# Two heads of 64 tokens in a gathered slot, and the weighted sum on the two column halves of the array

## The chip, the core and the metric

The kernel runs on one core of a Trainium2 chip. Its engines work beside each other and meet at semaphores: TensorE (PE in the profile; its weight loads are PEld), VectorE (DVE), ScalarE (ACT), GpSimd (POOL) and SyncE (SP, which only issues transfers here). Sixteen DMA engines move data between HBM and the core's memory. The metric is the device time of one execution in microseconds (us); less is better.

## The reference, cut to what matters

One layer of a streaming encoder on 1024 prompt tokens and 64 sample tokens, model width 1024. Two branches (a state-space scan and a causal convolution) are gated, merged and added to x. Then comes the part that this case is about: a mixture of 16384 tiny experts. For each token and each of 8 heads the best 16 experts are found from two sets of 128 keys, and each chosen expert contributes one row of `v_tab`, weighted by a softmax and by the gelu of a dot product with its row of `u_tab`:

```python
xn = rmsnorm(x, norm_ffn)
q = (xn @ w_q).reshape(tokens, 8, 2, 128)
s1, s2 = q[:, :, 0] @ keys1.T, q[:, :, 1] @ keys2.T        # tokens, heads, 128
v1, i1 = top_k(s1, 16); v2, i2 = top_k(s2, 16)
sc, pos = top_k(v1[..., :, None] + v2[..., None, :], 16)    # of 256 candidates
eidx = expert number of pos; g = softmax(sc)
coef = g * gelu(einsum('thkd,td->thk', u_tab[eidx], xn))
x = x + einsum('thk,thkd->td', coef, v_tab[eidx])
y = rmsnorm(x, norm_final)
```

All is float32. Every token takes 8 x 16 = 128 expert rows of 2 x 1024 numbers.

## The kernel before, in words

**Two streams of work.** The tokens pass through the layer (called `mix`) in 4 groups of 256 prompt tokens and 16 sample tokens, each group in 64 turns. The expert part (`peer`) works on tiles of 128 tokens: 8 prompt tiles and one tile with the 64 sample tokens. Group 0 runs `mix` alone. Then a loop of three passes runs `mix` of group g + 1 and `peer` of tiles 2g and 2g + 1 turn by turn. What is left, tiles 6, 7 and the sample tile (number 8), runs `peer` alone (`last_tiles`). In a turn k, PE has the products of the layer (L529 most of them; L547 and L557 in the scan stage, turns 10 to 25), then the expert work of four slots.

**A slot.** POOL gathers 128 rows of the expert table (u and v of an expert stand in one row of 8 KB), one per partition, by indices in `idx` (L1306). So a slot is 1 MB: the k-th expert of one head for 128 tokens. `rows` holds a ring of 8 slots. When a slot has landed, DVE multiplies its u half with the normed tokens `xn` and sums each row to one number in `dots` (L1199). For every two slots ACT takes the gelu (L809), DVE multiplies with the softmax weights (`coef`, L1186), and ACT writes for each slot a diagonal matrix `diag` (L812). PE multiplies `diag` with the v half of the rows and adds to `ps_acc` (L673): two matmuls of 512 columns each, with `diag` 128 x 128 as weights, so that `ps_acc` holds 128 tokens by 1024 columns. `slot_free` then lets POOL gather the next. Work is grouped by pairs of heads: a pair `n` has 32 slots, `a` = 0 or 1 says which of the two heads, and DVE chooses the experts of pair n + 1 (`key_top`, `pair_top`, `experts_of`) while pair n is summed, in eight turns.

**The sample tile** has 64 tokens. There the partitions hold two heads of 64 tokens already, `x2t` holds the tokens twice, and `fold` (two unit matrices one above the other) takes the place of `eye` in `diag`, which adds the two heads up.

**Begin and end of a tile.** `start` loads the tile's tokens (`x2t`, by SP), DVE makes `xn` (L1214), and PE puts x into `ps_acc` (L664). `end` waits for all slots: ACT squares `ps_acc` and sums (L825), DVE and ACT make the root (L1220, L827, L1222), and DVE writes `yt` (L1223). PE's `start` of the next tile waits for that. In mid group (turn 32) `end` of the even tile stands among DVE's work on the odd one.

**What sets the order.** The order on each engine is the order of the code; there is no scheduler. SP has one queue: the weight slabs of the layer (`ring`, four slots, L363), the scores that `mix` has stored (`sc`, L379), the tiles' tokens, and the stores of y. `HEAD_LOADS` says in which turns SP waits for the stored scores of a head before it loads them.

## Time and profile before

| | us |
|---|---|
| median of 3 runs | 3884.04 |
| lowest and highest | 3872.71, 3890.49 |
| span of the profiled execution | 3882.3 |
| PE busy | 3333.6 (86%) |
| DVE busy | 2776.0 (72%) |
| POOL busy | 1746.5 (45%) |
| ACT busy | 996.4 (26%) |
| mean granted clock of TensorE | 0.943 |

The profile gives no other time of the profiled execution than its span, from the first instruction to the last. Busy time is the time in which an engine has an instruction of the program at work; a PE record's end is modelled, so records overlap, and what a matmul costs in a row of them is read from the starts. A matmul in float32 leaves two records. The granted clock is 1.0 at 2.4 GHz and 0.5 at 1.2 GHz. The DMA share is the mean busy share of the sixteen DMA engines. By time the kernel has group 0 (0 to about 409 us, where the first slot is used), the loop (to about 3049) with a pass of about 880 us for each group, and the last tiles, which end about 3383, 3715 and 3882.

### The profile page before, as it was taken

What the parts mean: (1) busy time and instruction counts of PE and PEld (TensorE: products, weight loads), DVE (VectorE), ACT (ScalarE), POOL (GpSimd) and SP (SyncE); (2) the same over time, 40 slices, a digit from 0 to 9 for tenths busy, and PEclk for the clock granted to TensorE, in tenths of its full rate; (3) what the DMA queues carried; (4) which work ended last, traced back from release to release, by engine and by line L of the source; (5) the groups of instructions that cost most, each with busy time, mean ns of one, the idle gap of its engine ahead of it and who ended that gap; (6) DMA issues with size and microseconds to landing.
All of it is one profiled execution on the core that took longest, in us unless ns stands there. A gap on an engine that the chain in (4) does not pass through costs nothing.

```text
span 3882.3 us, 38138 instructions
## 1 busy us (share of the span) xinstructions
PE 3333.6 (86%) x9740; PEld 1810.3 (47%) x9740; DVE 2776.0 (72%) x6814; ACT 996.4 (26%) x2429; POOL 1746.5 (45%) x1548
## 2 busy tenths in 40 slices
PE   7878898898989799988999798888989777777777
PEld 5566454454555355454555354444545332233222
DVE  7952579997655569997655569997655677677775
ACT  1012233333222233333222233333222222212222
POOL 1600357744333347754333347854333344444443
PEclk9989999999999899999999899989999999999999
DMA  3235898899999898899999898889999999999998
GB/s 136 77 134 177 329 365 328 310 357 389 409 346 394 321 364 329 334 356 387 403 351 393 322 369 314 341 332 388 402 347 395 368 419 419 384 416 416 419 392 353
DMA packets 232123, 1337.74 MB, mean 345 GB/s; under 512 B 27936, under 2 KB 45472, under 8 KB 92656
## 3 DMA queue, kind: packets, MB, share of 16 engines
q0 software_dynamic: 156672, 1140.92, 74.0%
q1 hardware_dynamic: 63024, 181.13, 12.7%
q10 hardware_dynamic: 12224, 13.38, 1.0%
q8 instruction: 79, 1.29, 0.1%
q14 instruction: 124, 1.02, 0.1%
HBM read 1312.89 MB, written 22.44 MB: 344 GB/s over the span
## 4 chain that ended last, share of the span: by engine, by line
PE 39%; DVE 29%; DMA 15%; issue 11%; ACT 3%; POOL 3%; ACTq 0%; POOLq 0%; DVEq 0%; SPq 0%
PE ps_acc L673 22%; DMA rows<-in_experts,idx 15%; PE ps_a L529 11%; DVE rows L1199 9%; DVE va L1036 4%; PE ps_v L529 4%; POOL rows L1306 2%; DVE gp L1013 2%; DVE cand L1156 1%; DVE coef L1186 1%; DVE cand L1158 1%; PE ps_a L585 1%; DVE part L1160 1%; DVE rin L1002 1%; ACT diag L812 1%
## 5 line engine op out<-in xcount | busy, mean ns | idle before, releaser
L673 PE MATMUL ps_acc<-rows,diag 128*128 128x512 f32 x4352 | 2088.6, 633 | 427.7 <-ACT diag L812 427.7
L1306 POOL DMA_INDIRECT rows<-in_experts,idx x1088 | 1325.1, 1218 | 1864.1 <-PE ps_acc L673 1579.0
L1199 DVE CUSTOM_DVE_ANT_0 rows<-rows,xn 128x1024 f32<-128x1024 f32 x1088 | 1337.7, 1253 | 500.8 <-DMA rows<-in_experts,idx 494.3
L673 PEld LDWEIGHTS ps_acc<-rows,diag 128*128 128x128 f32 x4352 | 853.4, 202 | 1583.4 <-issue 946.1
L529 PE MATMUL ps_a<-xnT,ring 128*128 128x272 f32 x3072 | 747.0, 399 | 6.2 <-DMA ring<-in_slabs 2.7
L529 PEld LDWEIGHTS ps_a<-xnT,ring 128*128 128x128 f32 x3072 | 590.2, 193 | 186.8 <-issue 67.4
L812 ACT ACTIVATE diag<-pk,coef 128x128 f32<-128x128 f32 x1088 | 377.4, 394 | 1135.8 <-DVE coef L1186 1135.8
L809 ACT ACTIVATE act_v<-dots 128x2 f32<-128x2 f32 x544 | 110.5, 203 | 1122.3 <-DVE dots L1199 1118.4
L1036 DVE SCALAR_TENSOR_TENSOR va<-va,pk 128x302 f32<-128x302 f32 x480 | 258.8, 608 | 0.0
L1186 DVE TENSOR_TENSOR coef<-act_v,soft 128x2 f32<-128x2 f32 x544 | 109.7, 202 | 156.8 <-ACT act_v L809 126.0
L529 PE MATMUL ps_v<-uy,ring 128*128 128x272 f32 x512 | 129.0, 402 | 9.8 <-DVE uy L1103 9.8
L809 ACT ACT_TABLE_LOAD x100 | 128.3, 1283 | 13.9 <-issue 12.2
L529 PEld LDWEIGHTS ps_v<-uy,ring 128*128 128x128 f32 x512 | 100.2, 196 | 37.1 <-DVE uy L1103 10.1
L1013 DVE TENSOR_TENSOR_SCAN gp<-rho,carry,rin 128x256 f32<-128x256 f32 (+1 forms) x256 | 107.3, 481 | 0.0
L1199 DVE DVE_READ_ACCUMULATOR2_ANT dots<- 128x1 f32 x1088 | 89.1, 82 | 0.0
L547 PE MATMUL ps_v<-uy,bst 32*128 32x272 f32 x256 | 79.0, 421 | 10.9 <-DVE rot L1004 10.9
L557 PE MATMUL ps_y<-hst,cst 128*32 128x272 f32 x256 | 74.1, 414 | 9.3 <-POOL carry L1287 9.3
L1279 POOL TENSOR_TENSOR hst<-gp 128x272 f32<-128x272 f32 x64 | 72.7, 1136 | 9.4
L585 PE MATMUL ps_a<-pk,sig 128*128 128x128 f32 (+1 forms) x384 | 61.9, 284 | 17.2 <-ACT sig L792 17.2
L1129 DVE MAX8 topv<-sc 128x8 f32<-128x128 f32 x136 | 39.4, 289 | 41.1 <-DMA sc<-score_rows 40.9
L529 PE MATMUL ps_a<-uy,ring 128*128 128x272 f32 x256 | 65.9, 402 | 2.8 <-ACT uy L763 2.8
L792 ACT ACTIVATE sig<-ps_a 128x272 f32<-128x272 f32 x64 | 24.9, 389 | 164.6 <-PE ps_a L529 164.6
(188 smaller groups left out, 2214.3 us busy)
## 6 DMA issues: line engine op xcount, KB each, us to landing
ring<-in_slabs SPq DMA_DIRECT2D x260, 512.0 KB, 7.7
rows<-in_experts,idx POOLq DMA_INDIRECT x1088, 10.1
trig<-trig_rows SPq DMA_DIRECT2D x52, 272.0 KB, 2.9
sc<-score_rows SPq DMA_DIRECT2D x68, 128.0 KB, 6.9
score_rows<-uy ACTq DMA_DIRECT2D x32, 256.0 KB, 6.6
xt<-in_x_prompt SPq DMA_DIRECT2D x5, 1024.0 KB, 9.3
trig_rows<-rows SPq DMA_DIRECT2D x1, 4352.0 KB, 15.2
x_rows<-xt ACTq DMA_DIRECT2D x4, 1024.0 KB, 7.1
```

The source lines that it names most:

```text
L529: last = pe.matmul(out[:, 0:N], w, rhs[:, k, :], start=(k == 0), stop=(k == kt - 1))
L547: pe.matmul(out[:, 0:N], bst[q:q + 32, c, t, :], uT[q:q + 32, t, :], start=True, stop=True).then_inc(v_ready, 1)
L557: last = pe.matmul(ps_y[q:q + 32, 0:N], cst[:, c, j, :], hst[:, j % 2, c, :], start=(c == 0), stop=(c == 1))
L585: last = pe.matmul(out[0:width, t * KEYS:(t + 1) * KEYS], qT[:, m % 2, n:n + width], keys, start=True, stop=True)
L673: ins = pe.matmul(ps_acc[:, h, :], diag[:, slot, :], rows[:, slot, D + h * 512:D + (h + 1) * 512], start=False, stop=False, skip_group_che ...
L809: act.activation(act_v[:, cols], dots[:, cols], ACT.Gelu).then_inc(gelu_done, 1)
L812: act.activation(diag[:, s % RING, :], shape[0], ACT.Copy, scale=coef[:, s:s + 1]).then_inc(diag_done, 1)
L1013: last = dve.tensor_tensor_scan(grot[:, j % 2, p, lo:hi], rho[:, j:j + 1].to_broadcast([P, hi - lo]), rin[:, p, lo:hi], carry[:, p, j, str ...
L1036: last = dve.scalar_tensor_tensor(acc[:, c, :], src, wk, acc[:, c, :], ALU.mult, ALU.add)
L1186: dve.tensor_tensor(coef[:, cols], act_v[:, cols], flat(soft[:, :, :])[:, cols], ALU.mult).then_inc(coef_done, 1)
L1199: ins = dve.tensor_tensor_reduce(rows[:, slot, 0:D], rows[:, slot, 0:D], xn[:, :], 1.0, 0.0, ALU.mult, ALU.add, dots[:, s:s + 1])
L1306: pool.indirect_dma_start(out=rows[:, slot, :], out_offset=None, in_=experts, in_offset=bass.IndirectOffsetOnAxis(ap=idx[:, a, k:k + 1], a ...
```

## The change

A slot now holds two heads of 64 tokens for the prompt tiles too, as it did for the sample tile. `a`, which said which head of the pair, says now which half of the tile's tokens. For every slot `fold` (128 x 64) is scaled to a `diag` of 128 x 64, and its product has only 64 output rows. The two matmuls of a slot go to different halves of the array's columns: columns 0 to 511 of the result to partitions 0 to 63 of `ps_acc`, columns 512 to 1023 to partitions 64 to 127, both in the bank of the token half j. What follows from the new layout: `xn` is kept twice, for each token half on both partition halves (four operations on DVE instead of one); the sum of squares of a token is in two parts that DVE adds across the halves; `yt`, `gl` and the stores of y are in column halves; the scores of a slot's two heads are loaded by two transfers; and the score loads wait for pairs of heads (`PAIR_LOADS`).

```diff
-HEAD_LOADS = {TURNS - 10: 0, TURNS - 7: 1, TURNS - 2: 2}
+PAIR_LOADS = {TURNS - 10: 0, TURNS - 2: 1}
...
-        xn = sb("xn", [P, D])
+        xn = sb("xn", [P, 2, D])
-        yt = sb("yt", [P, D])
+        yt = sb("yt", [P, 2, DH])
-        diag = sb("diag", [P, RING, P])
+        diag = sb("diag", [P, RING, HT])
...
+        halves = (slice(0, HT), slice(HT, P))
+        def half_tiles(t):
+            return 1 if isinstance(t, int) and t == TILES else 2
+        def half_of(n, a):
+            return 0 if isinstance(n, int) and n >= TILES * TPAIRS else a
...
             def load_scores(n, a):
-                sp.dma_start(sc[:, a, :], score_d[2 * n + a]).then_inc(score_in[a], 16)
+                for f in range(2):
+                    sp.dma_start(sc[halves[f], a, :], score_d[2 * n + f, halves[a], :]).then_inc(score_in[a], 16)
...
-                sp.dma_start(y_t[t], yt[:, :]).then_inc(y_out, 16)
+                for f in range(2):
+                    sp.dma_start(y_t[t, f], yt[halves[f], :, :]).then_inc(y_out, 16)
...
-                    if k in HEAD_LOADS:
-                        h = HEAD_LOADS[k]
-                        sp.wait_ge(score_out[h % 2], 128 * g + 128 + 32 * (h // 2 + 1))
-                        pass_wait()
+                    if k in PAIR_LOADS:
+                        for b in range(2):
+                            sp.wait_ge(score_out[b], 128 * g + 128 + 32 * (PAIR_LOADS[k] + 1))
+                            pass_wait()
...
             def start(t):
-                for h in range(2):
-                    last = pe.matmul(ps_acc[:, h, :], eye[0:w, :], x2t[0:w, h * 512:(h + 1) * 512],
-                                     start=True, stop=False, skip_group_check=True)
+                for j in range(js):
+                    for f in range(2):
+                        last = pe.matmul(ps_acc[halves[f], j, :], eye[0:w, halves[j]], x2t[0:w, f * DH:(f + 1) * DH],
+                                         start=True, stop=False, skip_group_check=True)
...
             def peer(n, r, last=False):
                 for s in range(STEPS * r, STEPS * r + STEPS):
-                    slot = s % RING
+                    slot, j = s % RING, half_of(n, s // TOPK)
                     pe.wait_ge(diag_done, PAIR * n + s + 1)
-                    for h in range(2):
-                        ins = pe.matmul(ps_acc[:, h, :], diag[:, slot, :], rows[:, slot, D + h * 512:D + (h + 1) * 512],
+                    for f in range(2):
+                        ins = pe.matmul(ps_acc[halves[f], j, :], diag[:, slot, :],
+                                        rows[:, slot, D + f * DH:D + (f + 1) * DH],
                                         start=False, stop=False, skip_group_check=True)
                     ins.then_inc(slot_free, 1)
...
-                        act.activation(diag[:, s % RING, :], shape[0], ACT.Copy, scale=coef[:, s:s + 1]).then_inc(diag_done, 1)
+                        act.activation(diag[:, s % RING, :], fold, ACT.Copy, scale=coef[:, s:s + 1]).then_inc(diag_done, 1)
...
-                act.activation(yt[:, :], flat(ps_acc[:, :, :]), ACT.Square, accum_out=fin[:, 0:1]).then_inc(y_sq, 1)
+                for j in range(2):
+                    sq_j = act.activation(yt[:, j, :], ps_acc[:, j, :], ACT.Square, accum_out=fin[:, 0, j:j + 1])
+                sq_j.then_inc(y_sq, 1)
...
-                dve.scalar_tensor_tensor(xn[:, :], x2t[:, :], rst[:, 0:1], gf[:, :], ALU.mult, ALU.mult).then_inc(xn_ready, 1)
+                for j in range(half_tiles(t)):
+                    for f in range(2):
+                        last = dve.scalar_tensor_tensor(xn[halves[f], j, :], x2t[halves[j], :], rst[halves[j], 0:1],
+                                                        gf[halves[j], :], ALU.mult, ALU.mult)
+                last.then_inc(xn_ready, 1)
...
-                dve.tensor_scalar(fin[:, 1:2], fin[:, 0:1], 1.0 / D, EPS, ALU.mult, ALU.add).then_inc(y_ms, 1)
+                dve.tensor_scalar(fin[halves[0], 3, :], fin[halves[1], 0, :], 1.0 / D, EPS, ALU.mult, ALU.add)
+                step(dve.tensor_scalar(fin[halves[1], 3, :], fin[halves[0], 0, :], 1.0 / D, EPS, ALU.mult, ALU.add))
+                dve.scalar_tensor_tensor(fin[:, 1, :], fin[:, 0, :], 1.0 / D, fin[:, 3, :], ALU.mult, ALU.add).then_inc(y_ms, 1)
                 dve.wait_ge(y_std, 1 * t + 1)
-                step(dve.reciprocal(fin[:, 3:4], fin[:, 2:3]))
-                dve.scalar_tensor_tensor(yt[:, :], flat(ps_acc[:, :, :]), fin[:, 3:4],
-                                         gl[:, :], ALU.mult, ALU.mult).then_inc(y_ready, 1)
+                step(dve.reciprocal(fin[:, 3, :], fin[:, 2, :]))
+                for j in range(2):
+                    last = dve.scalar_tensor_tensor(yt[:, j, :], ps_acc[:, j, :], fin[:, 3, j:j + 1], gl[:, :],
+                                                    ALU.mult, ALU.mult)
+                last.then_inc(y_ready, 1)
```

The order of the instructions on PE stays. In the loop, turns 4 to 6, before (L529 are the layer's products, L673 a slot's two matmuls, the size is that of the result):

```order
229 L671 REGISTER_ALU
230 L673 MATMUL ps_acc<-rows,diag 128x512 x2
231 L510 REGISTER_ALU
232 L529 MATMUL ps_a<-xnT,ring 128x272 x8
233 L510 REGISTER_ALU
234 L529 MATMUL ps_a<-xnT,ring 128x272 x8
235 L671 REGISTER_ALU
236 L673 MATMUL ps_acc<-rows,diag 128x512 x2
237 L671 REGISTER_ALU
238 L673 MATMUL ps_acc<-rows,diag 128x512 x2
```

and the same place now, where L690 is the slot's line and L544 the layer's:

```order
229 L688 REGISTER_ALU
230 L690 MATMUL ps_acc<-rows,diag 64x512 x2
231 L525 REGISTER_ALU
232 L544 MATMUL ps_a<-xnT,ring 128x272 x8
233 L525 REGISTER_ALU
234 L544 MATMUL ps_a<-xnT,ring 128x272 x8
235 L688 REGISTER_ALU
236 L690 MATMUL ps_acc<-rows,diag 64x512 x2
237 L688 REGISTER_ALU
238 L690 MATMUL ps_acc<-rows,diag 64x512 x2
```

Nothing moved; the slots' products have 64 rows and stand between full ones of 128.

On DVE the end of a prompt tile in the last tiles and the begin of the next, before:

```order
L1220 TENSOR_SCALAR fin<-fin 128x1
L1222 RECIPROCAL fin<-fin 128x1
L1223 SCALAR_TENSOR_TENSOR yt<-ps_acc,fin,gl 128x1024
L1214 SCALAR_TENSOR_TENSOR xn<-x2t,rst,gf 128x1024
```

and now:

```order
L1240 TENSOR_SCALAR fin<-fin 64x2
L1241 TENSOR_SCALAR fin<-fin 64x2
L1242 SCALAR_TENSOR_TENSOR fin<-fin 128x2
L1244 RECIPROCAL fin<-fin 128x2
L1246 SCALAR_TENSOR_TENSOR yt<-ps_acc,fin,gl 128x512 x2
L1232 SCALAR_TENSOR_TENSOR xn<-x2t,rst,gf 64x1024 x4
```

Two small operations and three long ones are more than before, and `yt` is made in two pieces.

## Rows read from the trace of the kernel before

**Rows 1.** The page: busy time, and groups by line (count, busy us, mean ns, idle)
```profile
PE 3333.6 (86%) x9740; PEld 1810.3 (47%) x9740; DVE 2776.0 (72%) x6814; ACT 996.4 (26%) x2429; POOL 1746.5 (45%) x1548
...
L673 PE MATMUL ps_acc<-rows,diag 128*128 128x512 f32 x4352 | 2088.6, 633 | 427.7 <-ACT diag L812 427.7
...
L812 ACT ACTIVATE diag<-pk,coef 128x128 f32<-128x128 f32 x1088 | 377.4, 394 | 1135.8 <-DVE coef L1186 1135.8
```

**Rows 2.** Last tiles by stretches: length, busy PE, PEld, DVE, ACT, POOL; clock, DMA share, GB/s
```profile
3361.00:3392.00 31.00, 20.73 (x34) 7.81 (x35) 19.40 (x47) 9.32 (x21) 6.73 (x7) 0.78 0.88 352
3392.00:3703.00 311.00, 238.87 (x498) 95.14 (x497) 223.24 (x585) 63.33 (x193) 141.60 (x124) 0.96 1.01 414
3703.00:3725.00 22.00, 14.23 (x25) 5.30 (x24) 14.55 (x35) 8.09 (x16) 5.04 (x5) 0.77 0.78 320
```

**Rows 3.** Groups by line, 3392 to 3703 us: the dot products and their wait
```profile
L1199 DVE CUSTOM_DVE_ANT_0 rows<-rows,xn 128x1024 f32<-128x1024 f32 x123 | 149.0, 1225 | 71.8 <-DMA rows<-in_experts,idx 71.1 <-DVE soft L1180 0.6
```

**Rows 4.** One pass of the loop by stretches, columns as in Rows 2
```profile
1303.00:1334.00 31.00, 25.89 (x69) 11.46 (x69) 23.55 (x59) 8.78 (x26) 18.65 (x12) 0.94 0.97 378
1334.00:1421.00 87.00, 87.00 (x291) 55.45 (x290) 46.19 (x131) 26.19 (x56) 26.73 (x24) 0.98 0.94 362
1421.00:1728.00 307.00, 278.23 (x809) 149.80 (x809) 298.04 (x697) 100.07 (x194) 222.20 (x196) 0.94 0.89 339
1728.00:1756.00 28.00, 25.80 (x81) 14.98 (x80) 20.83 (x52) 10.81 (x21) 10.83 (x8) 1.00 0.98 378
1756.00:1962.00 206.00, 184.22 (x528) 98.05 (x526) 147.83 (x380) 53.40 (x138) 88.02 (x73) 0.97 0.99 399
1962.00:2022.00 60.00, 53.95 (x177) 31.73 (x178) 28.72 (x76) 13.36 (x43) 17.20 (x16) 0.94 0.89 308
2022.00:2131.00 109.00, 103.74 (x344) 61.57 (x343) 59.44 (x154) 24.66 (x80) 39.13 (x34) 0.97 0.98 397
2131.00:2182.00 51.00, 32.97 (x82) 15.96 (x81) 22.01 (x59) 14.92 (x36) 9.76 (x10) 0.80 0.74 282
```

**Rows 5.** The chain (start, us, what) and the timeline of PE, 1334 to 1421 us
```profile
1355.13 7.33 PE ps_a L529 x32
...
1348.10 7.03 PE L673 MATMUL ps_acc<-rows,diag 128*128 128x512 f32 x16
1354.97 7.50 PE L529 MATMUL ps_a<-xnT,ring 128*128 128x272 f32 x32
```

**Rows 6.** Timeline of PE in the scan stage (start us, us; 128x128, 32-row, 32-column)
```profile
709.46 3.83 PE L529 MATMUL ps_a<-xnT,ring 128*128 128x272 f32 x16
713.22 1.18 PE L547 MATMUL ps_v<-uy,bst 32*128 32x272 f32 x4
714.33 1.10 PE L557 MATMUL ps_y<-hst,cst 128*32 128x272 f32 x4
```

**Rows 7.** Groups by line and shape: narrow and full operands
```profile
L673 PEld LDWEIGHTS ps_acc<-rows,diag 128*128 128x128 f32 x4352 | 853.4, 202 | 1583.4 <-issue 946.1 <-ACT diag L812 632.2
L557 PE MATMUL ps_y<-hst,cst 128*32 128x272 f32 x256 | 74.1, 414 | 9.3 <-POOL carry L1287 9.3
L1117 DVE TENSOR_TENSOR xt<-xt,ps_v 128x512 f32<-128x512 f32 x16 | 10.2, 682 | 31.2 <-PE ps_v L645 31.1
L1117 DVE TENSOR_TENSOR xt<-xt,ps_v 16x512 f32<-16x512 f32 x8 | 5.1, 670 | 0.0
```

**Rows 8.** Timeline at the end of tile 6
```profile
3370.98 5.40 PE L673 MATMUL ps_acc<-rows,diag 128*128 128x512 f32 x8 [1.92 <-ACT diag L812]
3376.47 1.02 ACT L825 ACTIVATE yt<-ps_acc 128x1024 f32<-128x1024 f32 x1 [3.71 <-PE ps_acc L673]
...
3377.62 0.15 DVE L1220 TENSOR_SCALAR fin<-fin 128x1 f32<-128x1 f32 x1 [7.13 <-ACT yt L825]
...
3380.53 1.28 DVE L1214 SCALAR_TENSOR_TENSOR xn<-x2t,rst,gf 128x1024 f32<-128x1024 f32 x1
```

**Rows 9.** Timeline of SP before the first gather: the first score loads
```profile
353.36 0.91 SPq L379 DMA_DIRECT2D sc<-score_rows  x2
```

More of the change, by code:

```diff
@@ L30 @@
 HEADS, KEYS, TOPK = 8, 128, 16
+HT, DH = P // 2, D // 2
 EPS = 1e-6
@@ L197, in program @@
         coef = sb("coef", [P, PAIR])
-        diag = sb("diag", [P, RING, P])
-        fin = sb("fin", [P, 4])
+        diag = sb("diag", [P, RING, HT])
+        fin = sb("fin", [P, 4, 2])
         spare = rows[:, :, :].rearrange("p a b -> p (a b)")
@@ L301, in loads_of @@
         def loads_of(t):
-            return 16 * (TILES + 2) if isinstance(t, int) and t == TILES else 16 * t + 16
+            return 16 * t + 16
+        def half_tiles(t):
+            return 1 if isinstance(t, int) and t == TILES else 2
+        def half_of(n, a):
+            return 0 if isinstance(n, int) and n >= TILES * TPAIRS else a
         def angles(j, g):
@@ L428, in _ @@
                         sp.wait_ge(score_out[b], 32)
-                        load_scores(0, b)
+                    for a in range(2):
+                        load_scores(0, a)
                 if k == T_Q + 4:
@@ L450, in _ @@
                             pass_wait()
-                    if k in HEAD_LOADS:
-                        h = HEAD_LOADS[k]
-                        sp.wait_ge(score_out[h % 2], 128 * g + 128 + 32 * (h // 2 + 1))
-                        pass_wait()
+                    if k in PAIR_LOADS:
+                        for b in range(2):
+                            sp.wait_ge(score_out[b], 128 * g + 128 + 32 * (PAIR_LOADS[k] + 1))
+                            pass_wait()
                     if k == T_Q + 3:
@@ L481, in start @@
                     rows_free(t + 1)
-                    for f in range(2):
-                        half_tile = slice(f * DEC, (f + 1) * DEC)
-                        sp.dma_start(x2t[half_tile, :], x2_d[SEQ:SEQ + DEC, :]).then_inc(x2_in, 16)
-                        sp.dma_start(rst[half_tile, :], rs_d[SEQ:SEQ + DEC, :]).then_inc(rs_in, 16)
+                    sp.dma_start(x2t[0:DEC, :], x2_d[SEQ:SEQ + DEC, :]).then_inc(x2_in, 16)
+                    sp.dma_start(rst[0:DEC, :], rs_d[SEQ:SEQ + DEC, :]).then_inc(rs_in, 16)
             def end(t):
@@ L490, in end @@
                     pass_wait()
-                    sp.dma_start(y_sample.rearrange("b p d -> (b p) d"), yt[0:DEC, :]).then_inc(y_out, 16)
+                    for f in range(2):
+                        sp.dma_start(y_s[f], yt[halves[f], 0, :]).then_inc(y_out, 16)
                 else:
@@ L856, in _ @@
                         end(2 * g + 1)
-            last_tiles(act, start, peer, end)
+            last_tiles(act, lambda t: None, peer, end)
         @block.vector
@@ L1198, in peer @@
                     dve.wait_ge(landed[slot], 16 * (PAIR // RING * n + s // RING + 1))
-                    ins = dve.tensor_tensor_reduce(rows[:, slot, 0:D], rows[:, slot, 0:D], xn[:, :], 1.0, 0.0,
-                                                   ALU.mult, ALU.add, dots[:, s:s + 1])
+                    ins = dve.tensor_tensor_reduce(rows[:, slot, 0:D], rows[:, slot, 0:D], xn[:, half_of(n, s // TOPK), :],
+                                                   1.0, 0.0, ALU.mult, ALU.add, dots[:, s:s + 1])
                     if s % BATCH == BATCH - 1:
```

38 lines of the change are left out of this document (19 added, 19 removed).

## The prediction

> **What bounds the kernel now.** I read the page's waits and groups first, then the busy time by stretches, and took group 1 of the loop (1303 to 2182 us) as the pattern for all three. A slot is one gather of 128 expert rows, 1 MB; there are 1088 [rows 1].
>
> In the two tiles after the loop nothing but slots is left. There the sixteen DMA engines show a share of 1.01 at 414 GB/s while PE is busy 239 of 311 us [rows 2], and DVE waits 71 us for gathers [rows 3]. The DMA sets the pace, 311 us for 123 slots or 2.53 us each, and PE has a quarter of its time free.
>
> In the loop three things alternate [rows 4]. In 1334 to 1421 PE is busy 87.0 of 87 us and the chain is PE alone: 6.87 us of ps_acc for four slots, then 7.33 us of the layer's products, again and again [rows 5]. This is the stretch that the change addresses, and even here the DMA share is 0.94. In 1421 to 1728 (scan and taps) DVE is busy 298 of 307 us [rows 4], so DVE is the bound. In 1756 to 1962 the DMA share is 0.99. In 1962 to 2022 and 2022 to 2131 (scores and queries) PE is busy 158 of 169 us with DMA at 0.89 and 0.98. At the end of a group (2131 to 2182) nothing is busy: the tile drains.
>
> So PE looks like the bound by its 86% of the span [rows 1], but the DMA engines stand right behind it. What PE gives back can be no more than the DMA share that is missing where PE is the bound.
>
> **The slot's matmuls.** A slot costs four PE records now (two matmuls, each of two records: 4352 / 1088). They start 0.43 us apart, 16 of them 6.87 us [rows 5], so 1.72 us a slot. Afterwards the four records are 64 columns wide and alternate in pairs between the two column halves. If the halves work side by side, the second record of one half runs beside the first of the other, and a slot costs 0.86 us; four slots cost 3.86 us (one record of 0.43 is left over at the end). If they don't, it stays at 1.72. No row shows two products on different columns next to each other, so these are the two ends. A narrow product alone is no cheaper: the 32-column product L557 has 414 ns a record in the mean, and four of its records take 1.10 us like the full-width ones of L547 with 1.18 [rows 6, 7]. I take 0.86, for two reasons in the rows: the array does change its arrangement for narrow operands (the cost below), which it need not if narrow products were run like full ones, and the weight loads have room, four of 0.20 us being 0.81 us against 0.86 even at full width [rows 7]. This is the weakest choice of the working.
>
> The Trainium skill says the same in "TensorEngine Tiling (Array Packing)", section Key Properties: different tiles can load weights and multiply in parallel. No run here shows it yet.
>
> **Changing the arrangement.** In the scan stage the 16 full products from 709.46 take 3.76 us until the first 32-row product starts; at their own spacing (1.83 us per 8, from 7.33 us for 32) they would take 3.66. The four 32-row ones take 1.11 us to the next start where 4 x 0.229 is 0.92 [rows 6]. So a change costs 0.1 us before and 0.1 us after it, 0.2 in all. From 128x128 ps_acc to 128x128 products there is none: 1348.10 to 1354.97 is 6.87 us [rows 5]. After the change each turn that also has layer products has one change more (scan) or two (elsewhere): 0.4 us against 3.0 us saved.
>
> Here the skill speaks against the change: by the same page and section, changing the tiling mode drains TensorE. The trace agrees, and its price is the 0.2 us above.
>
> **What the PE gain is worth.** PE loses 3.0 - 0.4 = 2.6 us in each turn of 14.2 us (6.87 + 7.33), to 11.6. Four slots and two slabs by DMA then take 14.2 x 0.94 = 13.3 us if the share goes to 1. So the DMA is the bound at once, and a stretch gains its missing share, no more: 31 x 0.03 + 87 x 0.06 + 28 x 0.02 + 206 x 0.01 + 60 x 0.11 + 109 x 0.02 = 0.9 + 5.2 + 0.6 + 2.1 + 6.6 + 2.2 = 17.6 us a group [rows 4], 53 in three. Nothing in 1421 to 1728, where DVE is the bound, and nothing in the last tiles' steady part. I take three quarters, **-40 us**, since part of the missing share comes with the layer's serial steps. Upward the bound is the rate: were the loop's bytes to move at the 414 GB/s of the last tiles, the 87, 60, 109 and 206 us stretches could give 11 + 15 + 4 + 8 = 38 us a group, 114 in all. The 15 is from the stretch at 308 GB/s, where scores and rows are stored in small pieces and the share is 0.89 all the same, so I set the far end at 28 a group, 84.
>
> **The ends of the tiles.** The chain at 3371 to 3387 [rows 8]: last eight records, Square on ACT, fin on DVE, root, reciprocal, the yt product, then xn for the next tile, then the first slots. In it the DMA runs dry (share 0.88, 0.78) [rows 2].
> - Last batch of two slots: eight records at 0.43 us are 3.43 us now, and 4 x 0.43 + 0.43 = 2.15 us side by side: -1.3.
> - Square: two of 512 columns instead of one of 1024 (1.02 us; 1.15 from its start to fin's): half the time twice, and its fixed part, which is the part over the columns' time, once more: +0.25, an estimate from the 0.13 between the two numbers and a gap of the same size.
> - fin: three small DVE operations of about 0.15 instead of one, each after the other: +0.35. yt in two halves: +0.1.
> - xn: four operations on 64 partitions and 1024 columns. The same operation at 128 partitions is 1.28 us, and DVE's time goes by the columns: L1117 takes 682 ns on 128 partitions and 670 on 16 [rows 7]. So four cost 5.13: **+3.85**. All that could lower it is work that DVE would have waited for anyway; the low end is 0.
> - The first slot after it, four records at the low clock of 1.2 GHz (0.86 us each), frees its place one record earlier: -0.9.
>
> One such end in the last tiles: +2.35. The next (into the sample, where xn is two operations): +1.28 - 1.5 = -0.2. The last of all: -1.3 + 0.7 = -0.6. Ends of a group: four slots are queued, 6.87 to 3.86, so -3.0 + 0.2 + 0.7 + 3.85 - 0.9 = +0.85 each, three: +2.5. Tile ends in mid group (turn 32) have DVE idle 7 of 28 us and the DMA at 0.98 [rows 4], so of 4.3 us more DVE work I count 1.5, between 0 and 4.3: +4.5 for three.
>
> **Other edits.** Score loads are split in two DMAs of 64 partitions: SP issues one more each time, in about 0.45 us, behind nothing that is late. In turn 54 SP now waits for head 1's store instead of head 0's; queued behind it is the slab for a later turn, three slabs ahead, and DVE reads the scores two turns on: nothing. The first load has both heads stored already when it is issued (two L379 from 353.36 in 0.91 us) [rows 9]: +0.5 for the extra issue. diag is 64 columns instead of 128 on ACT (394 ns now), which waits 1136 us for coef anyway [rows 1]: nothing. The stores of y have twice the rows of half the length, beside other work. PE's copy of x2t into the sum (L664) has eight narrow records for four wide ones, so the same time side by side, under the longer xn.
>
> **Sum.** -40 + 2.5 + 4.5 + 2.35 - 0.2 - 0.6 + 0.5 = -31 us against the profiled span of 3882.3, which lies 1.7 us under the median of 3884.04: **3851 us**.
>
> **The rivals.** (a) The halves run one after the other. Then no PE time goes, 0.4 us is added in the roughly 22 turns a group where PE is the bound (+26 in three), and the tile ends cost their whole surplus: groups 3 x 4.75, mid-group 3 x 3, last tiles and sample about 8: +57, so 3939 us. For it: no row shows an overlap, and a 32-column record is as long as a full one. Against it: the cost of changing arrangement.
> (b) The halves overlap, but the missing DMA share belongs to the layer's steps and the DVE surplus at the tile ends is not hidden: a third of 53 gained, 3 x 4.3 in mid group: -18 + 16 = about 3880 us. For it: DMA is at 0.94 or above in most stretches already.
> (c) Slower by the clock. Where PE stands idle the granted clock falls: 0.78 and 0.80 in the tile ends, where PE is busy 21 of 31 and 33 of 51 us, against 0.95 to 0.98 in the dense stretches [rows 2, 4]. With half of the ps_acc time gone PE is idle more. In the last tiles this costs nothing: a batch of two slots at 1.2 GHz takes 3.9 us and the DMA brings two in 5.06. In the scan stage a turn keeps 3.66 + 1.1 + 1.1 + 3.86 us, 9.7 of about 15 us, and decides only if the mean clock there falls under 9.7 / 15 = 0.65 (now 0.94). At 0.5 a turn would be 19.4 us: 4.4 x 17 x 3 = +224 us, near 4070. At a clock between, nothing.
>
> **How the numbers follow.** The forecast 0.50, (b) 0.27, (a) 0.18, (c) 0.05. About 0.5% (19 us) is what a measurement of this kernel can tell from no change. The forecast is a gain of over 0.5% in nine of ten of its cases, and a few of (b) with it: faster 0.48. Same: the rest of these, 0.28. Slower: (a), (c): 0.24. The range goes from 3805 (84 us of gain, and the 9 for tile ends and loads paid: 3807) to 3925, the near side of (a); what is left out is (c), most of (a) and little else.
>
> **What would show it.** Four records of a slot start about 0.21 us apart in the mean, not 0.43, and 16 of them span 3.9 us; in 1334 to 1421 PE falls under 90% and the DMA share rises to 0.98 or more; the scan stage keeps its 257 us; the last two tiles keep 311 us between their ends; xn shows four rows of 1.28 us. The forecast is wrong if the records still start 0.43 us apart, if four xn operations don't stand on the path, or if the group falls well under 860 us, which would mean that the DMA share was no bound.

## The result and the profile after

The changed kernel takes 3910.88 us (median of six runs, 3895.58 to 3917.80), the kernel before 3877.15 us in six runs beside it. The ratio is 1.0074, with a 95% interval of 1.0054 to 1.0093: slower by 0.7%, where 3851 us and a gain of 0.8% were forecast. The time lies in the range given; its direction is the other one. That it lies in the range is luck: the upper end was set for halves that run one after the other, and that is not what happened. The profiled execution has a span of 3909.1 us at a mean granted clock of 0.826 (before: 3882.3 us and 0.943).

In the changed kernel L690 is the slot's matmul (L673 before), L1215 the dot product (L1199), L1052 the taps (L1036), L1330 the gather (L1306), L1299 to L1311 POOL's rotation (L1275 to L1287), L1232 xn and L1246 yt. The page, against [rows 1]:

```profile
PE 2729.4 (70%) x9772; PEld 1289.0 (33%) x9772; DVE 2877.2 (74%) x6866; ACT 936.9 (24%) x2447; POOL 1723.3 (44%) x1548
...
DVE 40%; DMA 25%; PE 16%; issue 13%; ACT 3%; POOL 2%; ACTq 0%; DVEq 0%; POOLq 0%; SPq 0%
...
L690 PE MATMUL ps_acc<-rows,diag 128*64 128x512 f32 x4352 | 1426.1, 797 | 1007.8 <-ACT diag L830 1007.6
...
L1052 DVE SCALAR_TENSOR_TENSOR va<-va,pk 128x302 f32<-128x302 f32 x480 | 321.4, 736 | 0.0
```

PE is busy 604 us less. DVE is busy 101 us more, though the diff gives it only a few operations per tile. The taps alone are 63 us of it (321.4 us, 258.8 before). The chain that ended last is now DVE's before all others. The timeline of PE in the stretch where PE was the bound, against [rows 5]:

```profile
1354.29 3.65 PE L690 MATMUL ps_acc<-rows,diag 128*64 128x512 f32 x16
1357.88 7.60 PE L544 MATMUL ps_a<-xnT,ring 128*128 128x272 f32 x32
1365.41 3.65 PE L690 MATMUL ps_acc<-rows,diag 128*64 128x512 f32 x16
```

The sixteen records of four slots take 3.59 us to the next start (1354.29 to 1357.88) where they took 6.87: the column halves run side by side (an experiment below puts both products on one half, and then the same records take 7.01 us). So the time was not lost in the matmuls. The stretches of one pass of the loop and of the last tiles, columns as in [rows 2] and [rows 4]:

```profile
1342.00:1427.00 85.00, 77.37 (x322) 47.13 (x320) 52.92 (x144) 24.79 (x56) 31.56 (x32) 0.96 1.02 414
1427.00:1720.00 293.00, 196.10 (x654) 85.36 (x655) 284.95 (x596) 81.61 (x164) 204.82 (x180) 0.80 0.82 304
...
2040.00:2156.00 116.00, 89.98 (x372) 47.20 (x368) 66.30 (x174) 24.00 (x86) 43.50 (x38) 0.93 1.00 404
...
3420.00:3722.00 302.00, 177.37 (x484) 39.34 (x480) 218.25 (x570) 55.80 (x189) 144.71 (x122) 0.71 1.00 413
```

In the first, PE fell to 91% and the DMA share rose to 1.02. The second is the scan stage: DVE is busy 285 of 293 us, and the DMA share is down to 0.82. The same stage of the kernel before:

```profile
1426.00:1693.00 267.00, 238.23 (x673) 123.91 (x672) 259.20 (x597) 85.47 (x164) 205.37 (x184) 0.93 0.89 337
```

DVE executes 597 instructions there before and 596 now, and needs 26 us more for them.

The table gives the time between the first dot products of the turns, from their starts in the two traces, in us for each of the three groups (turns 10 to 27 are the scan stage; 31 to 33 and 63 hold the ends of the tiles):

```
turns               before                 after                  mean change
0 to 3              41.6   42.0   41.9     42.0   40.0   40.2     -1.1
4 to 9              91.2   91.3   89.2     83.8   84.1   83.5     -6.8
10 to 27 (scan)    274.1  266.6  274.1    292.0  293.0  291.0    +20.4
28 to 30            37.0   37.2   37.6     37.3   37.4   37.4     +0.1
31 to 33            36.3   36.7   36.8     39.4   38.4   39.7     +2.6
34 to 49           188.4  190.6  189.5    189.9  189.5  189.2      0.0
50 to 62           179.0  177.7  178.9    171.5  170.7  171.8     -7.2
63                  35.9   35.9   30.9     37.5   38.0   33.8     +2.2
after the loop     333.6, 332.0, 153.1    333.3, 331.4, 151.4    -2.6 in all
```

The last row has tile 6, tile 7 and the sample tile up to its last dot product. The change gives 14 us a group where PE was the bound, costs 5 at the tile ends, and loses 20.4, or 61 in three groups, in a stage that the prediction said would not move. (The prediction took group 1 as the pattern for all. Its scan stage, 266.6 us, was the shortest of the three already.)

### The profile page after: what moved, and what is told of

It is laid out like the page before. It is cut to its first block, busy times and chain, and to the rows that moved or that the text cites. A ratio compares the mean times of both kernels' runs of the same rounds, so it can differ in the third digit from the quotient of the medians.

```text
span 3909.1 us, 38486 instructions
## 1 busy us (share of the span) xinstructions
PE 2729.4 (70%) x9772; PEld 1289.0 (33%) x9772; DVE 2877.2 (74%) x6866; ACT 936.9 (24%) x2447; POOL 1723.3 (44%) x1548
## 3 DMA queue, kind: packets, MB, share of 16 engines
q14 instruction: 125, 1.02, 0.1%
## 4 chain that ended last, share of the span: by engine, by line
DVE 40%; DMA 25%; PE 16%; issue 13%; ACT 3%; POOL 2%; ACTq 0%; DVEq 0%; POOLq 0%; SPq 0%
DMA rows<-in_experts,idx 25%; DVE rows L1215 14%; PE ps_acc L690 7%; DVE va L1052 7%; PE ps_a L544 6%; DVE gp L1029 2%; POOL rows L1330 1%; DVE cand L1174 1%; DVE cand L1172 1%; DVE part L1176 1%; DVE coef L1202 1%; ACT diag L830 1%; DVE xn L1232 1%; PE ps_v L544 1%; DVE rin L1018 1%
## 5 line engine op out<-in xcount | busy, mean ns | idle before, releaser
L690 PE MATMUL ps_acc<-rows,diag 128*64 128x512 f32 x4352 | 1426.1, 797 | 1007.8 <-ACT diag L830 1007.6
L1330 POOL DMA_INDIRECT rows<-in_experts,idx x1088 | 1275.9, 1173 | 1908.0 <-PE ps_acc L690 1616.1
L1215 DVE CUSTOM_DVE_ANT_0 rows<-rows,xn 128x1024 f32<-128x1024 f32 x1088 | 1364.0, 1275 | 500.2 <-DMA rows<-in_experts,idx 493.6
L690 PEld LDWEIGHTS ps_acc<-rows,diag 128*64 128x64 f32 x4352 | 338.2, 171 | 1988.0 <-ACT diag L830 1545.5
L544 PE MATMUL ps_a<-xnT,ring 128*128 128x272 f32 x3072 | 765.5, 405 | 6.4 <-DMA ring<-in_slabs 2.9
L544 PEld LDWEIGHTS ps_a<-xnT,ring 128*128 128x128 f32 x3072 | 584.3, 194 | 250.1 <-issue 122.3
L830 ACT ACTIVATE diag<-pk,coef 128x64 f32<-128x64 f32 x1088 | 319.2, 340 | 1122.8 <-DVE coef L1202 1122.8
L1052 DVE SCALAR_TENSOR_TENSOR va<-va,pk 128x302 f32<-128x302 f32 x480 | 321.4, 736 | 0.0
L1202 DVE TENSOR_TENSOR coef<-act_v,soft 128x2 f32<-128x2 f32 x544 | 95.7, 176 | 136.8 <-ACT act_v L827 104.3
L544 PE MATMUL ps_v<-uy,ring 128*128 128x272 f32 x512 | 137.1, 421 | 20.4 <-DVE uy L1119 20.4
L544 PEld LDWEIGHTS ps_v<-uy,ring 128*128 128x128 f32 x512 | 103.8, 205 | 56.2 <-issue 23.2
L1215 DVE DVE_READ_ACCUMULATOR2_ANT dots<- 128x1 f32 x1088 | 87.5, 80 | 0.0
L1308 POOL TENSOR_TENSOR hst<-gp 128x272 f32<-128x272 f32 x64 | 82.4, 1287 | 5.0
L681 PE MATMUL ps_acc<-x2t,pk 128*64 128x512 f32 (+1 forms) x68 | 28.5, 981 | 65.7 <-DVE yt L1246 65.7
L544 PE MATMUL ps_a<-uy,ring 128*128 128x272 f32 x256 | 67.2, 407 | 3.1 <-ACT uy L781 2.8
```

What stands on the lines that cost most here:

```text
L544: last = pe.matmul(out[:, 0:N], w, rhs[:, k, :], start=(k == 0), stop=(k == kt - 1))
L690: ins = pe.matmul(ps_acc[halves[f], j, :], diag[:, slot, :], rows[:, slot, D + f * DH:D + (f + 1) * DH], start=False, stop=False, skip_gro ...
L830: act.activation(diag[:, s % RING, :], fold, ACT.Copy, scale=coef[:, s:s + 1]).then_inc(diag_done, 1)
L1052: last = dve.scalar_tensor_tensor(acc[:, c, :], src, wk, acc[:, c, :], ALU.mult, ALU.add)
L1202: dve.tensor_tensor(coef[:, cols], act_v[:, cols], flat(soft[:, :, :])[:, cols], ALU.mult).then_inc(coef_done, 1)
L1215: ins = dve.tensor_tensor_reduce(rows[:, slot, 0:D], rows[:, slot, 0:D], xn[:, half_of(n, s // TOPK), :], 1.0, 0.0, ALU.mult, ALU.add, dot ...
```

## What became slow in the scan stage

Groups by line in the scan stage: dot products and taps of the kernel before (1426 to 1692.5 us),

```profile
L1199 DVE CUSTOM_DVE_ANT_0 rows<-rows,xn 128x1024 f32<-128x1024 f32 x72 | 92.8, 1326 | 0.4 <-DVE soft L1180 0.4
...
L1036 DVE SCALAR_TENSOR_TENSOR va<-va,pk 128x302 f32<-128x302 f32 x96 | 47.9, 565 | 0.0
```

and of the changed kernel (1426.8 to 1719.8 us):

```profile
L1215 DVE CUSTOM_DVE_ANT_0 rows<-rows,xn 128x1024 f32<-128x1024 f32 x73 | 106.9, 1499 | 0.4 <-DVE soft L1196 0.4
...
L1052 DVE SCALAR_TENSOR_TENSOR va<-va,pk 128x302 f32<-128x302 f32 x96 | 67.7, 771 | 0.0
```

Each is the same operation on the same number of elements. The dots take 14 us more and the taps 20; `coef` and a few others take less, so that DVE's sum is 26. A timeline of a turn tells which of them grow. First the kernel before, one turn from the first dot product on (start us, duration us):

```profile
1470.70 2.08 POOL L1306 DMA_INDIRECT rows<-in_experts,idx  x1 [0.38 <-issue]
1470.76 1.22 DVE L1199 CUSTOM_DVE_ANT_0 rows<-rows,xn 128x1024 f32<-128x1024 f32 x1
...
1471.90 1.22 DVE L1199 CUSTOM_DVE_ANT_0 rows<-rows,xn 128x1024 f32<-128x1024 f32 x1
...
1472.80 0.93 POOL L1275 TENSOR_TENSOR gp<-gp,trig 128x272 f32<-128x272 f32 x1
...
1473.05 1.77 DVE L1199 CUSTOM_DVE_ANT_0 rows<-rows,xn 128x1024 f32<-128x1024 f32 x1
...
1473.70 1.74 POOL L1276 TENSOR_TENSOR gp<-gp,trig 128x272 f32<-128x272 f32 x1
```

Beside a gather a dot takes 1.22 us. The third dot, beside POOL's rotation, takes 1.77. Now a turn of the changed kernel:

```profile
1502.99 1.01 PE L690 MATMUL ps_acc<-rows,diag 128*64 128x512 f32 x2
1503.17 1.10 POOL L1330 DMA_INDIRECT rows<-in_experts,idx  x1 [0.76 <-PE ps_acc L690]
1503.59 0.87 DVE L1029 TENSOR_TENSOR_SCAN gp<-rho,carry,rin 128x256 f32<-128x256 f32 x2
...
1504.38 3.61 DVE L1052 SCALAR_TENSOR_TENSOR va<-va,pk 128x302 f32<-128x302 f32 x4
1504.83 1.32 POOL L1330 DMA_INDIRECT rows<-in_experts,idx  x1 [0.55 <-issue]
1506.17 0.77 POOL L1299 TENSOR_TENSOR gp<-gp,trig 128x272 f32<-128x272 f32 x1
1506.89 0.76 POOL L1300 TENSOR_TENSOR gp<-gp,trig 128x272 f32<-128x272 f32 x1
...
1507.91 1.77 DVE L1215 CUSTOM_DVE_ANT_0 rows<-rows,xn 128x1024 f32<-128x1024 f32 x1
1508.68 1.62 POOL L1305 TENSOR_TENSOR gp<-gp,trig 128x272 f32<-128x272 f32 x1
...
1509.62 1.77 DVE L1215 CUSTOM_DVE_ANT_0 rows<-rows,xn 128x1024 f32<-128x1024 f32 x1
...
1510.27 1.73 POOL L1306 TENSOR_TENSOR gp<-gp,trig 128x272 f32<-128x272 f32 x1
...
1511.32 1.76 DVE L1215 CUSTOM_DVE_ANT_0 rows<-rows,xn 128x1024 f32<-128x1024 f32 x1
```

The rotation began 2.04 us after the first dot before (1472.80 against 1470.76); here it begins 1.74 us ahead of it (1506.17 against 1507.91). It lies beside the taps, which take 3.61 us instead of 1.84 for four, and beside three dots of 1.77 us. Both engines pay: beside the dots a POOL operation takes 1.62 to 1.73 us, where the rotation's first two here take 0.77 and 0.76. Dots and POOL's operations follow each other in one rhythm of 1.70 us, the 1.15 between the starts of two undisturbed dots and 0.55 more, as if they took turns at something that both need.

The four taps are one line above. A narrower window (1505.8 to 1507) shows the last of them by itself:

```profile
1505.70 2.29 DVE L1052 SCALAR_TENSOR_TENSOR va<-va,pk 128x302 f32<-128x302 f32 x1
```

The first three take 0.51 to 0.53 us. The fourth takes 2.3 and ends only after the first two POOL operations, neither of which is longer than its 0.77. So one tap can lose 1.8 us. In the three scan stages together 31 of 288 taps take 2.1 us or more and 51 about 1.0 us; in the kernel before it is 7 and 7. The taps' durations add up to 62 us more than before and the dots' to 25 more, while `coef`, `rin` and the choice of experts lose about 30 us of such growth. The net is 57 us of the stage's 61.

Why earlier? POOL rotates a turn once it has issued the gathers of the turn before, and these wait for slots that PE has to free. In this turn PE is through with them at 1504.0, before DVE begins the taps, and the last two gathers go out at 1503.2 and 1504.8; the rotation follows at once. This turn is the common case now. By the starts in the traces, the rotation begins ahead of the turn's first dot in 39 of the 48 turns, where it did so in 9 of 48 before; the median start is 2.7 us ahead of it, and was 2.1 us after it.

That gave the **theory**: PE, twice as fast, lets POOL's rotation start earlier, onto DVE's operations with two operands in SBUF, and both engines then wait for each other. **Rival 1**: the granted clock (0.93 before, 0.80 now in this stage) makes PE late in the stage, and DVE's times are a by-product. **Rival 2**: the narrow matmuls or the new layout of xn and the slots make the dot itself dearer, wherever POOL's rotation lies.

## The experiments

Ratios are against the kernel before, run on the same chip beside each (medians of 3879.0 to 3880.1 us). Differences of a few us between kernels run on different chips are less certain than the ratios.

**POOL's rotation later.** In the scan stage POOL waits, before it rotates, until the turn's four dots are done. The edit is the same in both kernels:

```diff
                 for k in range(TURNS):
+                    if T_SSM <= k < T_SSM + PAIRS:
+                        pool.wait_ge(dots_done, PB * (GPAIRS * g + k // PTURNS) + TB * (k % PTURNS) + TB)
                     mix(k, g + 1)
```

In the changed kernel:

> The changed kernel with one wait more: in the scan stage POOL begins the rotation of a turn (seven small operations) only after DVE has done the four dot products of that turn. Theory P (POOL against DVE): DVE is the bound of the scan stage, and each of its two-input operations that meets POOL's rotation is 0.5 us longer; the faster matmuls free the slots earlier, so POOL starts the rotation earlier and meets taps and dot products. Then the scan stage goes from 292 us a group to 272 or less, and the kernel from 3911 to 3800 to 3855 us. Theory C (clock and latency of PE): the scan stage is longer because the granted clock fell there from 0.94 to 0.84. Then the wait changes nothing, or makes it longer: 3905 to 3930.

In the kernel before:

> The kernel before with the same wait of POOL in the scan stage. Theory P: there too some dot products and taps were long (mean 1326 and 565 ns in that stage against 1222 and 525 beside nothing), about 12 to 15 us a group: 3840 to 3870 us. Theory C: nothing moves, 3877.

Measured: the changed kernel with it 3797.09 us (ratio 0.9793, 0.9780 to 0.9807), the kernel before with it 3836.0 us (0.9890, 0.9875 to 0.9905). A wait *added* to POOL makes the changed kernel about 110 us faster (114 by the medians, on two chips) and the kernel before 43. Both are a little faster than the forecasts. The scan stage takes 256.6 us in the one and 256.3 in the other. In it, for the changed kernel, stretch and groups:

```profile
1384.00:1641.00 257.00, 188.10 (x655) 83.07 (x656) 249.33 (x597) 81.61 (x164) 178.35 (x183) 0.87 0.92 350
```

```profile
L1215 DVE CUSTOM_DVE_ANT_0 rows<-rows,xn 128x1024 f32<-128x1024 f32 x73 | 86.5, 1221 | 0.4 <-DVE soft L1196 0.4
...
L1052 DVE SCALAR_TENSOR_TENSOR va<-va,pk 128x302 f32<-128x302 f32 x96 | 45.4, 539 | 0.0
```

Dots are back at 1221 ns and taps at 539, with the new layout and the narrow matmuls in place: rival 2 falls. POOL's own busy time fell by 26 us too. The granted clock in this stage is 0.87 in the changed kernel with the late rotation and 0.97 in the kernel before with it, and the stage takes the same: rival 1 falls. Freed from the meeting, the change is worth 3836 - 3797 = **39 us**.

**The halves one after the other.** Both matmuls of a slot go to the first column half, so that they can't overlap; POOL's and DVE's code is that of the changed kernel.

```diff
-                        ins = pe.matmul(ps_acc[halves[f], j, :], diag[:, slot, :],
+                        ins = pe.matmul(ps_acc[halves[0], j, :], diag[:, slot, :],
```

In the changed kernel as it is:

> The changed kernel, but both products of a slot go to column half 0 of the array (the second half of the output is left out, so y is not computed). The records of a slot then can't run side by side. PE is as slow as before the change, or slower by the changes of arrangement. Theory P: POOL is late again, the scan stage comes back to about 272 us, and what is left are the longer tile ends and less room in the PE-bound turns: 3885 to 3915 us, with a scan stage that is shorter than in the changed kernel although PE is slower. Theory C: the clock comes back to 0.94, but PE's work doubles; scan stage about as before; this run alone doesn't tell them apart. If column halves brought nothing, the time stays at 3911.

And on top of the late rotation:

> The changed kernel with the late rotation, but both products of a slot on column half 0 (half of y is left out). The rotation is out of play, so this prices the side by side work alone. Theory: the gain of running side by side is the 40 us between 3836 and 3797 plus what the longer tile ends and the changes of arrangement cost, some 35 to 50 us: 3870 to 3890 us, with the scan stage at 256 us a group as in both kernels with the late rotation.

Measured: 3942.97 us (1.0159, 1.0138 to 1.0180) and 3888.71 us (1.0021, 1.0007 to 1.0034). The same sixteen records take 7.01 us to the next start now:

```profile
1358.07 7.08 PE L690 MATMUL ps_acc<-rows,diag 128*64 128x512 f32 x16
1365.08 7.60 PE L544 MATMUL ps_a<-xnT,ring 128*128 128x272 f32 x32
```

The second time is at the upper end of what was forecast. The first was forecast at 3885 to 3915 and missed by 28 us: its scan stage came back to near the 272 expected, but the longer tile ends and the turns with a slow PE cost more than was put down for them (53 us, by the two kernels with the late rotation: 3889 - 3836). The first is the link of the theory that the late rotation alone doesn't show. PE is slow again, and the scan stage goes back from 292 to 276.1, 274.6 and 277.5 us, with 1395 and 599 ns for the operations that the changed kernel has at 1499 and 771:

```profile
L1215 DVE CUSTOM_DVE_ANT_0 rows<-rows,xn 128x1024 f32<-128x1024 f32 x73 | 99.3, 1395 | 0.4 <-DVE soft L1196 0.4
...
L1052 DVE SCALAR_TENSOR_TENSOR va<-va,pk 128x302 f32<-128x302 f32 x96 | 51.1, 599 | 0.0
```

The rotation begins ahead of the turn's first dot in 13 of 48 turns again (39 in the changed kernel), and 10 taps are long instead of 31. So it is PE's speed, and nothing in DVE's or POOL's code, that moves the rotation onto the taps. With the rotation late in both, one half against two is worth 3889 - 3797 = 92 us, and the scan stage is 256.5 us either way.

**Nearly no rotation.** POOL's rotation works in the loop on 16 of 272 columns. In the changed kernel and in the kernel before:

```diff
-                mark(pool.tensor_tensor(prod[:, 0, :], grot[:, b, 0, :], c, ALU.mult))
+                mark(pool.tensor_tensor(prod[:, 0, 0:e], grot[:, b, 0, 0:e], c[:, 0:e], ALU.mult))
```

and so on for the other five operations.

> The changed kernel with POOL's rotation cut to 16 of 272 columns in the loop's groups (the scan's output is not right, so the rest is left out). It prices all meetings of POOL's arithmetic with DVE. Theory P: dot products go to 1222 ns and taps to 525 in the scan stage, 292 us to about 250, the kernel to about 3790. Theory C: the scan stage stays near 290 us.

> The kernel before with POOL's rotation cut to 16 of 272 columns in the loop's groups (the scan's outputs are left out). Theory P: the scan stage falls from 272 us a group to the 242 us that the changed kernel has with the same cut, so about 3790 us, and the difference between this kernel and the changed one with the cut (3748) is what the change is worth when nothing meets on DVE: about 40 us. If the halves brought less than that, this would be near 3760.

Measured: 3747.66 us (0.9658, 0.9643 to 0.9673) and 3791.22 us (0.9773, 0.9753 to 0.9792); the scan stage takes 242.4 and 241.9 us. No dot and no tap in the stage is lengthened by more than 0.1 us. Against this the late rotation still has about 14 us a group, 0.8 a turn of the 18, at `coef`, `rin` and the candidates. The first of the two was forecast at about 3790 us and came out 42 lower: it gained 163 us, of which 149 in the scan stage, where 126 had been counted. The change is worth 44 us here, by a second way and without an added wait.

Over the kernels so far the scan stage follows DVE's durations. Both are sums over the three groups, in us; the durations add up to more because the records overlap at their ends:

```
                                scan stages   DVE's durations
small rotation, before / after  725.6 / 727.2    797 / 796
late rotation, before / after   769.0 / 769.9    841 / 843
before                          814.8            887
one half                        828.2            899
after                           876.0            944
```

The difference between the columns is 68 to 73 us in every row. What the stage gains or loses is how long DVE's instructions take, and their number is the same.

**The rotation in the middle.** It waits for the first two dots instead of four (`+ 1` for `+ TB` in the edit above).

> The changed kernel with a rotation that waits for the first two of a turn's four dot products, not for all. Theory P by dose: two dot products of 16 turns meet the rotation and are 0.55 us longer each, taps none: scan stage about 257 + 17 = 270 to 275 us a group, near that of the kernel before, and 3840 to 3850 us. If what matters is only that POOL keeps off the taps, 3800.

Measured: 3801.49 us (0.9804, 0.9782 to 0.9826) and 259.0 us for the stage. I had expected 3840 to 3850, since two dots still lie beside the rotation. The timeline of one turn shows why they don't pay:

```profile
1477.39 1.22 DVE L1215 CUSTOM_DVE_ANT_0 rows<-rows,xn 128x1024 f32<-128x1024 f32 x1
...
1477.64 1.59 POOL L1299 TENSOR_TENSOR gp<-gp,trig 128x272 f32<-128x272 f32 x1 [0.51 <-DVE dots L1215]
...
1478.54 0.71 DVE L1202 TENSOR_TENSOR coef<-act_v,soft 128x2 f32<-128x2 f32 x1
1479.17 1.22 DVE L1215 CUSTOM_DVE_ANT_0 rows<-rows,xn 128x1024 f32<-128x1024 f32 x1
1479.19 1.82 POOL L1300 TENSOR_TENSOR gp<-gp,trig 128x272 f32<-128x272 f32 x1
```

Here whichever begins second waits. POOL's first operation begins inside a dot, waits for its end, and holds up only the tiny coef behind it (0.71 us instead of 0.16). Its second begins 0.02 us after the last dot and ends when DVE has gone on to operations that don't mind. So DVE pays 0.55 us once in this piece of the turn. The mistake was to price a meeting by the operations that overlap; as far as dots and coef show it, DVE pays where a POOL operation was already waiting when DVE's next one came. In the late version DVE pays at a coef of 0.71 us as well, and the whole stage is only 2.4 us a group longer with the rotation in the middle.

**Fewer xn operations, and the better version.** With the rotation late, first only two of the four xn operations of a tile (and xn cleared once before the loop):

```diff
-                    for f in range(2):
+                    for f in (j,):
                         last = dve.scalar_tensor_tensor(xn[halves[f], j, :], x2t[halves[j], :], rst[halves[j], 0:1],
```

> The changed kernel with the late rotation (3797 us), and of the four operations that make xn only the two that stay on their own partition half (xn on the other half is left out, so y is not computed). It prices the two crossing operations, 2 x 1.28 us at each of eight tile starts. If all of it stands on the path: 3797 - 20 = 3777. If DVE would have waited anyway in mid group and after the loop: about 3787.

Then x2t loaded once for each half of the partitions, so that xn is again made of two operations on 128 partitions, with nothing left out:

```diff
-                    for f in range(2):
-                        last = dve.scalar_tensor_tensor(xn[halves[f], j, :], x2t[halves[j], :], rst[halves[j], 0:1],
-                                                        gf[halves[j], :], ALU.mult, ALU.mult)
+                    last = dve.scalar_tensor_tensor(xn[:, j, :], x2t[:, j, :], rst[:, j:j + 1],
+                                                    gf[:, :], ALU.mult, ALU.mult)
```

> The changed kernel with the late rotation, and the tile's tokens loaded twice (once for each partition half), so that xn takes two operations on 128 partitions instead of four on 64; it costs 0.5 MB more by DMA at each tile, 1.3 us at the rate of the last tiles. DVE saves 2.6 us at each tile start: 3797 - 8 x 1.3 = about 3787 us; if the DMA takes back all of it, 3797.

Measured: 3774.74 us (0.9734, 0.9715 to 0.9752) and 3781.29 us (0.9750, 0.9733 to 0.9768). The two operations saved give 22 us, near the 20 of the case that all of it stands on the path; the second copy of x2t takes 6 us of that back, which is within the spread of either. The second of these kernels computes everything and beats both the kernel before (by 2.5%) and the changed one.

**Later still.** The same kernel, with the rotation waiting for the turn's last coef:

> As the kernel with two copies of the tokens (3781 us), but POOL's rotation waits for the last coef of the turn instead of its last dot product, so it begins 2 to 4 us later, beside DVE's products from PSUM and the scan, and may reach the taps. Theory P: what still meets the rotation (256 us a group against 242 with the small rotation) moves from coef and cand to rin and the taps: between 3765 (if it meets less) and 3820 us (if each turn's four taps meet it, 16 x 4 x 0.5 us less what is saved). A look for the best place, with no theory that excludes either.

Measured: 3833.43 us (0.9889, 0.9864 to 0.9913), 52 us worse and above the range that was forecast. The dots stay at 1218 ns, but now the rotation meets the next turn's scan. Group over the stage (1389.9 to 1663.4 us) and one turn:

```profile
L1032 DVE TENSOR_TENSOR_SCAN gp<-rho,carry,rin 128x256 f32<-128x256 f32 (+1 forms) x60 | 43.2, 778 | 0.0
```

```profile
1461.67 0.76 POOL L1307 TENSOR_TENSOR gp<-gp,trig 128x272 f32<-128x272 f32 x1
1461.83 0.90 DVE L1025 TENSOR_TENSOR rin<-rot 128x272 f32<-128x272 f32 x1
1462.39 0.95 POOL L1308 TENSOR_TENSOR gp<-gp,trig 128x272 f32<-128x272 f32 x1
1462.65 2.63 DVE L1032 TENSOR_TENSOR_SCAN gp<-rho,carry,rin 128x256 f32<-128x256 f32 x4
```

The scan takes 778 ns where all other kernels have 480 to 483. Of the places tried, the best for the rotation is thus neither early nor late but beside the choice of experts, whose MAX8 and FIND_INDEX8 keep their durations in all of these kernels.

## Why the prediction was wrong

**The step that failed** is "Nothing in 1421 to 1728, where DVE is the bound". An engine that is the bound was taken to have a fixed time. Its 298 us of work [rows 4] already held some 0.1 us for each dot (1326 ns in this stage, 1225 in the last tiles [rows 3]) for meeting POOL (with the rotation late the kernel before has them at 1218 ns), and this part depended on when PE freed the slots. The term was 0 and measured +61 us in the three groups. None of the rivals had it either; the slower side was given to serial halves and to the clock.

The Trainium skill, "SBUF — State Buffer", section "Who interferes with whom", has a rule that the prediction didn't weigh: a VectorE instruction with two SBUF inputs contends with a GpSimd instruction that reads SBUF, over ports that one of them holds for its whole instruction while the other is blocked. The trace agrees on who pays: dot, tap, scan, rin and coef have two inputs in SBUF and grow; the rotations' products that read PSUM and the MAX8 don't; nor does a dot beside a gather (1.22 us). On the order it agrees for dots and coef. For the long taps it doesn't show it: they begin 0.3 to 0.5 us ahead of POOL's first product by their recorded starts, and wait for two products all the same. The price is 0.5 to 0.55 us for DVE in most meetings and up to 1.8 us in the long taps, and 0.8 to 1.0 us for a POOL operation that waits.

Point by point, otherwise:

- **Halves side by side: right.** "16 of them span 3.9 us": 3.65, with 3.59 to the next start. Rival (a), serial halves, was put at 3939 us: the kernel with one half took 3943. That fit is partly chance, since 13 us of it are in the scan stage, which (a) did not count. The clean comparison is with the rotation late in both: 53 us (3889 - 3836) against the 57 of (a).
- **Changing the arrangement, 0.2 us: consistent.** Between the starts there is 3.59 us for 16 records (8 x 0.43 is 3.44), and 7.53 for the layer's 32 where 7.33 stood before. In both are 0.35 us, a little less than the 0.4 counted.
- **What the PE gain is worth: right where PE was the bound.** The DMA share went to 1.02 and 1.00, as said, so the DMA was the next bound. Turns 4 to 9 gained 6.8 us a group and turns 50 to 62 gained 7.2, 42 us in all; the term was 53, of which three quarters were taken, 40.
- **Tile ends: too small.** Group ends +2.2 us each (0.85 said), mid-group ends +2.6 (1.5 said): 14 us instead of 7. xn's own price was right, four operations in 5.16 us:

```profile
3405.96 1.41 DVE L1246 SCALAR_TENSOR_TENSOR yt<-ps_acc,fin,gl 128x512 f32<-128x512 f32 x2
3407.29 5.16 DVE L1232 SCALAR_TENSOR_TENSOR xn<-x2t,rst,gf 64x1024 f32<-64x1024 f32 x4
```

  The prediction summed xn's surplus to 21 us (3.85 at four ends, 1.5 at three, 1.28 at one), and leaving half of it out gave 22. The trace with only two of the operations says where: it is 1.7 us shorter in turns 31 to 33 and 2.5 in turn 63, of the 2.56 that two operations cost. So in mid group xn's share was set too low (1.5 us for three operations more, where two already cost 1.7). At the group ends it was priced right, and what was too generous were the savings set against it; that is inferred and was not tried by itself.
- **Last tiles keep their time: right.** 333.3 and 331.4 us (333.6 and 332.0 before), in the steady part 120 dots in 302 us, 2.52 us a slot (2.53 before). The +2.35 us for the end of a tile there did not show.
- **Clock, rival (c): the clock fell, the time didn't follow.** The granted clock is 0.71 in the last tiles (0.96 before) with PE busy 177 of 302 us, and 0.80 in the scan stage. It would have decided below 0.65 there.

Without the meeting the forecast sum, -31 us, stands against -39 and -44 measured. The mechanisms summed were right in sign; the one not summed was twice as large.

**Open.** The kernel before has 274, 267 and 274 us in the scan stage and the one-half kernel 276, 275 and 278 although PE is about as slow in both. By the durations this rest, 13 us in all, is again growth of DVE's instructions (12 us, 7 of them taps). What shifts the rotation there was not tried; xn's layout and the changes of arrangement are both possible. Why a tap that begins before POOL's product waits for two of them is not shown by any run either.

## What to carry to other kernels

A bound engine's time is not a constant: before writing "nothing changes here", list its operations with two inputs in SBUF, what POOL does beside them, and what sets POOL's start; if the edit makes an engine faster that releases POOL, the overlap moves. A mean that differs between stages for the same shape (1326 against 1225 ns) was the mark of such a meeting here, and it could be read before the change was made. The remedy may be a wait: holding POOL's rotation back until the four dots are done turned a loss of 0.7% into a gain of 2.1%.

## What the hardware showed that was not expected

- A DVE operation that meets one of POOL's arithmetic operations grows by 0.5 to 0.55 us, short or long: coef from 0.16 to 0.71, the dot from 1.22 to 1.77. POOL's operation grows from 0.77 to 1.6 to 1.8 us when it is the one that waits.
- A meeting can cost more than that: a tap of 0.53 us took 2.3 while two POOL operations of 0.77 ran one after the other. 31 such taps against 7 before are some 41 us in three groups, the largest part of the loss.
- Two inputs in SBUF are not the only mark: the small shift and mask that make `hilo` have one input tensor, and a few of them took 0.72 us instead of 0.17 beside a waiting POOL operation (5 in the kernel before, 12 with the rotation in the middle).
- For dots it matters who waits and not who overlaps: with POOL starting 0.02 us after a dot, the dot keeps its 1.22 us.
- Two 64-column products on the two column halves run at nearly twice the pace in fp32: 16 records in 3.59 us against 7.01 on one half and 6.87 at full width, with 0.35 us for the changes of arrangement in a turn.
- Halving the time of the slot matmuls (PE busy 3334 to 2729 us) took the mean granted clock from 0.943 to 0.826, and no stretch was seen in which this set the time.
